# Weighing a pair of heads behind the next pair's scores, and turning probabilities in the middle of a unit

## What is computed

```python
def hybrid_mixer(h, cos, sin, w_in, b_in, rel_bias, w_branch, w_out):
    proj = h @ w_in + b_in                      # qa ka va | qi ki wi | qkv_b | qkv_c f_c | gate_logits
    ...
    o_a = dsa_attention(qa, ka, va, qi, ki, wi) # 6 heads, keys chosen by top-k of 8 index heads' scores
    o_b = chunk_band_attention(...)             # 5 heads, relative bias
    o_c = forgetting_attention(...)             # 5 heads, decaying mask
    gates = jax.nn.sigmoid(gate_logits.reshape(B, S, N_BRANCH, D))
    y = (gates[:, :, 0] * (o_a @ w_branch[:WIDTH_A])
         + gates[:, :, 1] * (o_b @ w_branch[WIDTH_A:WIDTH_A + WIDTH_B])
         + gates[:, :, 2] * (o_c @ w_branch[WIDTH_A + WIDTH_B:]))
    return y @ w_out
```

## Time and profile before

| | |
|---|---|
| time, median of three runs | 1458.31 us (1455.73 to 1458.57) |
| profiled execution, its span | 1455.9 us |
| PE busy | 1434.6 us (99%) |
| PEld, ACT busy | 1202.6 (83%), 756.6 (52%) |
| DVE, POOL busy | 723.7 (50%), 1211.2 (83%) |
| chain that ended last | PE 93%, DVE 3%, ACT 1%, POOL 1% |
| attention of layer 0, of layer 1 (from the start) | about 112 to 226 us, 541 to 655 us |

### The profile page before, as it was taken

The page is one execution under the profiler, slowest core; times in us unless marked ns, Lnnn a source line. Parts: engine busy times, 40 slices in busy tenths (PEclk is TensorE's granted clock), DMA queues, the critical chain, the costliest instruction groups (busy, mean ns, idle before and its releaser), DMA issues.

```text
span 1455.9 us, 21556 instructions
## 1 busy us (share of the span) xinstructions
PE 1434.6 (99%) x7600; PEld 1202.6 (83%) x7600; DVE 723.7 (50%) x1556; ACT 756.6 (52%) x1275; POOL 1211.2 (83%) x986
## 2 busy tenths in 40 slices
PE   7999999999999999999999999999999999999997
PEld 5898777799988987778888888778888888788886
DVE  7863654766643754745566304454650044655202
ACT  4435675644445345765544445674654346665442
POOL 3799989898878987559898997966999977789995
PEclk9999999999999999999999999999999999999999
DMA  9994556689875986337676565644556655445561
GB/s 362 397 357 160 187 171 229 227 306 316 315 266 162 399 310 214 114 99 231 221 243 201 187 204 171 188 142 145 188 188 202 217 163 184 130 162 201 194 197 58
DMA packets 149559, 313.35 MB, mean 215 GB/s; under 512 B 10934, under 2 KB 31818, under 8 KB 149451
## 3 DMA queue, kind: packets, MB, share of 16 engines
q1 hardware_dynamic: 147696, 310.62, 63.0%
q10 hardware_dynamic: 1756, 1.35, 0.3%
HBM read 310.87 MB, written 1.06 MB: 214 GB/s over the span
## 4 chain that ended last, share of the span: by engine, by line
PE 93%; DVE 3%; ACT 1%; POOL 1%; issue 1%; DMA 1%; SPq 0%; POOLq 0%; DVEq 0%; ACTq 0%
PE bank L804 58%; PE bank L849 12%; PE bank L850 8%; PE bank L847 5%; PE bank L1012 1%; PE bank L996 1%; POOL lo_units L741 1%; PE bank L885 1%; PE bank L982 1%; DMA x_rows<-in_x 1%; PE bank L1095 1%; PE bank L1064 1%; PE bank L1028 1%; PE bank L1111 1%; PE bank L1054 0%
## 5 line engine op out<-in xcount | busy, mean ns | idle before, releaser
L741 POOL TENSOR_TENSOR lo_units<-raw_units,hi_units 128x512 fp32r<-128x512 f32 (+3 forms) x928 | 1151.0, 1276 | 223.7 <-ACT hi_units L1390 222.7
L1390 ACT ACTIVATE hi_units<-raw_units 128x1024 fp32r<-128x1024 f32 (+1 forms) x470 | 482.8, 1031 | 410.5 <-PE bank L804 248.6
L804 PE MATMUL bank<-hi_units,turned 128*128 128x512 f32 (+3 forms) x1600 | 441.7, 391 | 2.1 <-DVE turned L1928 1.7
L804 PEld LDWEIGHTS bank<-hi_units,turned 128*128 128x128 f32 x1600 | 291.9, 189 | 53.7 <-issue 3.3
L850 PE MATMUL bank<-turned,lo_units 128*128 128x256 f32 x1024 | 288.4, 282 | 0.0
L804 PE MATMUL bank<-hi_units,turned_wide 128*128 128x512 f32 x992 | 274.6, 391 | 0.0
L849 PE MATMUL bank<-turned,hi_units 128*128 128x512 f32 x736 | 260.1, 398 | 0.0
L804 PE MATMUL bank<-lo_units,turned 128*128 128x512 f32 (+3 forms) x800 | 253.5, 384 | 0.8 <-POOL lo_units L741 0.5
L804 PEld LDWEIGHTS bank<-hi_units,turned_wide 128*128 128x128 f32 x992 | 185.3, 188 | 38.5 <-issue 0.5
L850 PEld LDWEIGHTS bank<-turned,lo_units 128*128 128x128 f32 x1024 | 194.5, 190 | 0.2
L804 PEld LDWEIGHTS bank<-lo_units,turned 128*128 128x128 f32 x800 | 150.2, 189 | 30.8 <-POOL lo_units L741 3.7
(11 more groups left out here) (266 smaller groups left out, 1294.3 us busy)
## 6 DMA issues: line engine op xcount, KB each, us to landing
ada_units<-in_ada_w SPq DMA_DIRECT2D x88, 512.0 KB, 7.4
raw_units<-in_w_ffn_tiles SPq DMA_DIRECT2D x72, 512.0 KB, 5.2
raw_units<-in_mlp_w_out SPq DMA_DIRECT2D x64, 512.0 KB, 3.3
raw_units<-in_mlp_w_tiles SPq DMA_DIRECT2D x56, 512.0 KB, 3.3
raw_units<-in_w_in SPq DMA_DIRECT2D x56, 458.0 KB, 9.7
raw_units<-in_w_in SPq DMA_DIRECT2D x48, 512.0 KB, 6.9
raw_units<-in_w_ffn_out SPq DMA_DIRECT2D x44, 512.0 KB, 4.0
raw_units<-in_moba_w_qkv SPq DMA_DIRECT2D x24, 512.0 KB, 3.7
```

The lines of the kernel that those rows point to most:

```text
L741: pool.tensor_tensor(LO[:, s, b, 0:w], RAW[:, u["slot"], b, 0:w], HI_[:, s, b, 0:w].bitcast(F32), ALU.subtract).then_inc(lo_ready.sem, lo_ ...
L804: ins = pe.matmul(BANK[2 * c["pair"] + t][:, 0:w], (A[a] if A is BT else A[:, a])[:, part, t * P:(t + 1) * P], W[:, s, b, 0:w], start=(i = ...
L1390: act.activation(HI_[:, s, 0:n, 0:w], RAW[:, u["slot"], 0:n, 0:w], ACT.Copy)\
```

## The change

- TensorE: `weigh_pair` of a pair moves from the middle of the unit in the even step (its odd head + 3) to the next, odd step, right behind the scores of the next pair and ahead of the unit. In step 25 there are no scores and it stands at the step's start; the last pair is weighed behind the loop, after the unit of step 26.
- TensorE: `turn_head(k-3)` moves from ahead of the unit to between its two blocks, up to step 24. In steps 25 and 26 it stays ahead. `branch_unit` takes `amid` so that this holds in step 24 too.
- ScalarE: `pair_hi` moves from the end of the even step to the next odd step, between `even_probs` and exp; the last one is behind the loop.
- VectorE: `pair_lo` moves from `late` of the even step (ahead of the top-k round) to the next odd step, between the mask and `copy_turned`; the last one is behind the loop.

```diff
@@ tensor, attention
-            for k in range(len(heads) + pipe["weigh"]):
+            last_step = len(heads) + pipe["weigh"] - 1
+            for k in range(last_step + 1):
                 h = k - pipe["score"]
                 if 0 <= h < len(heads) and h % 2 == 0:
...
+                if k <= last_step - 1:
+                    weigh_pair(k - pipe["weigh"] - 1)
                 if k < len(heads) and k % 2 == 0:
...
+                if k <= len(heads):
+                    weave(k, lambda: turn_head(k - pipe["turn"]))
+                    continue
                 turn_head(k - pipe["turn"])
-                weave(k, lambda: weigh_pair(k - pipe["weigh"]))
+                weave(k, None)
+            weigh_pair(len(heads) - 1)
@@ tensor, weave
-                    branch_unit(l, *c, u)
-                    amid()
+                    branch_unit(l, *c, u, amid)
@@ scalar, attention
                 if HI <= k - pipe["score"] - 1 < len(heads):
                     even_probs(tag, k - pipe["score"] - 1)
+                h = k - pipe["weigh"] - 1
+                if h >= HI and h % 2:
+                    pair_hi(tag, h)
...
-                h = k - pipe["turn"]
-                if h >= HI and h % 2:
-                    pair_hi(tag, h)
+            pair_hi(tag, len(heads) - 1)
@@ vector, attention
+                h = k - pipe["weigh"] - 1
+                if real(h) and h % 2:
+                    outputs(h)
                 copy_turned(k - pipe["turn"])
-                late(k, outputs)
+                late(k)
+            outputs(len(heads) - 1)
@@ vector, late
-                if h >= HI and h % 2:
-                    pair_out(h)
```

More of the change, by code:

```diff
@@ L1274, in weave, with branch_unit @@
                     c, u = (((0, "C"), 0), ((0, "C"), 1), ((1, "C"), 0))[k - 4 * N_GATE]
-                    branch_unit(l, *c, u)
-                    amid()
-            def branch_unit(l, cc, b, u):
+                    branch_unit(l, *c, u, amid)
+            def branch_unit(l, cc, b, u, amid=None):
                 pe.wait_ge(turned_lo.sem, turned_lo.at((("o", l), {"C": (3, 4), "B": (1, 2), "A": (N_PAIRS - 2, N_PAIRS - 1)}[b][u])))
-                unit(by_key["branch", l, cc, b], u, HT if b == "A" else BT)
+                unit(by_key["branch", l, cc, b], u, HT if b == "A" else BT, amid=amid)
             def forget_products(l, c):
@@ L2228, in weave, with late @@
                     dve.wait_ge(act_side.sem, act_side.at(("bias mask", l)))
-            def late(k, pair_out, l=l):
+            def late(k, l=l):
                 if k == HI + HB + ONE["score"] + 1:
@@ L2242, in late @@
                     tell(v.tensor_tensor(GATES[:, 1, j * CW:(j + 1) * CW], banks[1][:, :], b, ALU.add), drained, key)
-                h, r = k - ONE["weigh"], k - (HI + 2)
+                r = k - (HI + 2)
                 if r == TOPK // 8:
                     link(v.tensor_scalar(IDX[:, :], IDX[:, :], PICKED, NEG, ALU.not_equal, ALU.mult))
-                if h >= HI and h % 2:
-                    pair_out(h)
                 if 0 <= r < TOPK // 8:
```

## The result

| | before | after |
|---|---|---|
| time, median of six runs | 1457.53 us | 1465.16 us |
| lowest to highest | 1455.73 to 1462.70 | 1463.60 to 1468.44 |
| profiled execution, its span | 1455.9 | 1464.5 |
| PE, DVE, ACT busy | 1434.6, 723.7, 756.6 | 1439.0, 722.6, 756.5 |

The changed kernel is slower: ratio 1.0052, interval 1.0040 to 1.0065, +7.6 us. The forecast was 1461.1 us with a range of 1455.0 to 1464.0; the time lies above that range. Three single executions of the later comparisons, at 1719, 2001 and 5007 us, are left out of every median and ratio.

A forecast was written before the change was run, and what follows sets the result against it. TensorE, busy 74.47 of some 75 us a stretch, was taken to bound the kernel. Per layer -0.96 - 0.75 + 3.13 = +1.42 us, two +2.84, on the median 1458.31: 1461.1 us, range 1455.0 to 1464.0.

The forecast's parts named there:

- weighing behind scores, six pairs: TensorE, odd steps 13 to 23: three changes of array shape instead of four save 0.16 us a pair, -0.96 a layer.
- stops of steps 16 and 26: TensorE's old waits for VectorE's copy of probabilities (0.33 us) and for ScalarE (0.42) both go: -0.75 us a layer.
- stop of step 13: TensorE waits for `pair_lo` before turning: chain with a drain 5.56 us against 4.73 of TensorE work, stop 0.83 us.
- stop of step 17: TensorE waits for `pair_lo` of a pair in two tiles: chain 10.57 us against 8.27 of work, stop 2.30 us.
- Part 4: New TensorE wait for `pair_lo` before turning head k-3 in odd steps, priced by chaining VectorE and ScalarE: +3.13 us a layer.
- the weighing itself never waits: Rival case: weighing stops for the odd head's copy; no time of its own. Neutral form of the change: 1459.0 us, chance 0.07.
- The rival without a new stop: `pair_lo` ends within TensorE's work at steps 13 and 17, only the savings stay: -3.4 us, 1454.9, chance 0.14.
- the one with a stop in every odd step: Margin of 0.42 us at steps 15, 19, 21, 23 vanishes, stops up to 0.4 us each: +3.1 on top, 1464.2, chance 0.09.
- The link from `pair_lo`'s end to TensorE's start: Last link of the VectorE and ScalarE chain to TensorE's turn in odd steps, put at 0.05 us.
- The junction: TensorE's direct change from scores (64x128) to weighing (128x64), in no earlier row: 0.16 us saved, both sections together 1.84 us.
- Part 2: Turning probabilities between the unit's blocks on TensorE: same three full-shape transposes, 0.33 us in either place, so no cost by itself.

The follow-up runs named there:

- the last comparison: The changed kernel, unaltered, run once more beside the kernel before to see its spread: ratio 1.0038 (1.0024 to 1.0053).
- two swaps in the other engines' order: Changed kernel with, on ScalarE, `pair_hi` ahead of `even_probs`: ratio 1.0004; separately, with VectorE's top-k round ahead of `copy_turned`: ratio 1.0001.

## Why the prediction was wrong

Per layer, in us:

| term | forecast | measured |
|---|---|---|
| weighing behind scores, six pairs | -0.96 | -0.65 |
| stops of steps 16 and 26 | -0.75 | -0.76 |
| stop of step 13 | +0.83 | +0.94 |
| stop of step 17 | +2.30 | +2.37 |
| sum | +1.42 | +1.90 (stretch +1.92) |
| clock at half behind the stop of step 17 | not there | +1.58 where it falls |

- **The step that failed** is the end of Part 4: a stop was priced at its own length. "Queued behind the waiting instruction on TensorE is all its work" was said, but not that this work may then run at 1.2 GHz. No rival had it either. Layer 1 and layer 0 of the profiled execution lost 1.58 us each to it, 3.2 us in all; with it the forecast's own sum would have been 1464.3. Rows 1 gave the granted clock as full, and the prediction took it to stay so after its own new stop of 2.3 us. Without the fall the terms come to +3.8 us for both layers, where the forecast had +2.8. How far the time lies from the forecast hangs on how often the clock falls: in the last comparison the same kernel had a median of 1463.17, inside the range.
- **Mechanism and places** were right: chain and stops of steps 13 and 17, in both layers, at `pair_lo`; no stop elsewhere; the old two gone; the weighing itself never waits. The rival without a new stop is refuted by the waits, the one with a stop in every odd step as well: steps 15 and 19 to 23 have none.
- **The two stops** were forecast 0.11 and 0.07 us too short. The link from `pair_lo`'s end to TensorE's start is 0.15 us at both (169.37 + 0.42 to 169.94; 188.36 + 0.86 to 189.37), where 0.05 was put.
- **The junction.** L982 starts 0.20 us after the last scores. Counted as in the prediction, with the late start of the products behind (165.53 + 0.23 to 167.51, and 0.10), the two sections cost 1.86 us; the forecast was 1.84. They cost 2.00 before. Leaving 64x128 costs the same 0.20 us from start to start, whether 128x64 follows or 128x128 (167.59 to 167.79 before), as was taken. But the two-step period shrank from 8.62 us (190.24, 198.85, 207.48: the low products ahead of the weighing) to 8.52 (195.79, 204.31, 212.82), by 0.108 and not by 0.16, which gives the -0.65 for six pairs. Part 2 is why, at least in part: turning inside the unit was costed at nothing, but a block right behind another takes 1.37 us (204.43 to 205.80 before) and one behind a turn 1.39, and now no two blocks stand together. So 0.31 us less was saved a layer than forecast. With an error of this size alone, and the two stops as measured, the time would have been in the range.
- **The median** was 1458.31 at first and 1457.53 with three runs more, which moves the forecast by less than 1 us.

## What to carry to other kernels

Price a new stop of an engine that otherwise never stands by more than its length: ask what its clock is granted afterwards, and shorten the stop until it lies below every length behind which a profiled execution showed a fall (here none behind 1.5 to 1.7 us, three of four behind 2.4) before looking for more savings. When a consumer is moved ahead of its producer's queue, chain the producer's queue from the last time that it was idle; two swaps in the other engines' order (what is ready first, goes first) took 2.9 and 3.5 us a layer off the changed kernel, each alone, where the move itself is worth 1.5. And don't give a late producer time by delaying, in every step, the work that starts its chain.

## What the runs showed of the hardware

- The granted clock fell from 2.4 to 1.2 GHz after a stop of 2.4 us of an otherwise busy TensorE in three of four cases in the profiled executions, 0.45 to 1.3 us after the stop had ended, and in two of two with a stop of 2.96 us, there 0.5 to 0.6 us before it had ended. With stops of 1.5 to 1.7 us, six cases, it didn't. Each time it stayed at half for 3.41 us and then was full again. With the stop filled by unused products it stayed full in two of two. The Trainium skill, "TensorE: Matmul & The Clock Gate", Why this matters for your kernels, advises against idle gaps between bursts of matmuls, since the clock then falls back to half; these runs agree, and here one fall cost 1.58 us.
- From the last pass of a split shape to the first of the next shape the starts lie 0.20 us apart, where 0.10 lie between two passes of one shape: 166.51 to 166.71 from scores to weighing, 167.31 to 167.51 from weighing to L804. From a 512-column product into a split shape it is 0.33 instead of 0.23 (165.53 to 165.86). The Trainium skill, "TensorEngine Tiling (Array Packing)", Key Properties, says "Mode switching requires drain"; the direct junction, which no row of before had, agrees in that it isn't free: it starts 0.20 us on, too.
